# Earlier rounding of the first down weights, activations by token half, two sums postponed, and two gate stretches in the last attention pair

## The reference, cut to what matters

```
h = RMSNorm(x) * (1 + scale1) + shift1
p = h @ W_in
o_b = mixer_b(p slice)      b in {RG-LRU, stick-breaking attention, gated DeltaNet, RWKV-7}
x = x + gate1 * ( sum_b sigmoid(h W_gate_b + b_gate_b) * (o_b W_branch_b) ) @ W_out
h = RMSNorm(x) * (1 + scale2) + shift2
x = x + gate2 * ConvFFN(h)
out = RMSNorm(x)

ConvFFN(h) = (gelu(causal_conv3(h @ w_gate)) * (h @ w_up)) @ w_down      # 2816 hidden channels
```

## Time and profile before

| | |
|---|---|
| median of 3 runs | 1860.83 us (1860.56, 1860.83, 1863.67) |
| the profiled execution, its own time | 1862.51 us |
| its span, first to last instruction | 1860.7 us |
| mean granted TensorE clock | 0.995 |
| PE busy | 1821.3 us (98%) |
| DVE, POOL, ACT busy | 1132.7 (61%), 828.0 (44%), 589.1 us (32%) |

### The profile page before, as it was taken

How to read it: one execution, slowest core, us unless ns; L and a number is a source line. 1 busy time by engine, 2 the same in 40 slices (tenths; PEclk the granted TensorE clock), 3 DMA queues, 4 the chain that set the end, 5 groups by cost and what they waited for, 6 DMA issues and landing times.

```text
span 1860.7 us, 34460 instructions
## 1 busy us (share of the span) xinstructions
PE 1821.3 (98%) x14030; PEld 1458.8 (78%) x14030; DVE 1132.7 (61%) x1706; ACT 589.1 (32%) x957; POOL 828.0 (44%) x954
## 2 busy tenths in 40 slices
PE   6999999999999999999999999999999999999997
PEld 4778777767888888878878788878888888888885
DVE  4855568844555455465544653986666556665656
ACT  4341344352213122222131422543222332233223
POOL 2767556523242233222232747155454455455443
PEclk9999999999999999999999999999999999999999
DMA  9616211224120221230214551011022111111012
GB/s 339 221 46 237 91 62 57 87 95 128 50 91 25 87 95 39 76 104 35 78 55 174 190 215 46 23 46 59 33 68 68 45 45 45 68 45 58 33 68 91
DMA packets 72029, 163.55 MB, mean 88 GB/s; under 512 B 6112, under 2 KB 30816, under 8 KB 71904
## 3 DMA queue, kind: packets, MB, share of 16 engines
q1 hardware_dynamic: 64416, 142.88, 22.5%
q10 hardware_dynamic: 7488, 18.88, 2.6%
HBM read 133.17 MB, written 28.57 MB: 87 GB/s over the span
## 4 chain that ended last, share of the span: by engine, by line
PE 88%; DVE 6%; issue 2%; POOL 2%; ACT 1%; DMA 1%; SPq 1%; ACTq 0%; DVEq 0%; POOLq 0%
PE gbank L782 35%; PE gbank L1339 17%; PE mbank L1440 11%; PE mbank L1123 3%; PE mbank L1339 3%; PE gbank L1263 1%; PE gbank L1323 1%; PE gbank L1353 1%; PE mbank L1353 1%; DVE fa L2384 1%; POOL w_lo L650 1%; PE gbank L1123 1%; PE mbank L863 1%; PE mbank L1043 1%; PE gbank L884 1%
## 5 line engine op out<-in xcount | busy, mean ns | idle before, releaser
L646 POOL TENSOR_TENSOR w_hi<-w_raw,zero 128x256 fp32r<-128x256 f32 (+1 forms) x260 | 203.1, 811 | 618.7 <-PE gbank L782 598.1
L782 PE MATMUL gbank<-h_hi,w_hi 128*128 128x512 f32 x976 | 392.7, 402 | 0.2 <-POOL w_lo L650 0.2
L782 PE MATMUL gbank<-h_hi,w_lo 128*128 128x512 f32 x976 | 389.2, 399 | 0.0
L782 PE MATMUL gbank<-h_lo,w_hi 128*128 128x512 f32 x976 | 384.3, 394 | 0.0
L696 POOL TENSOR_TENSOR ra<-late,ra 128x256 fp32r<-128x256 f32 x208 | 187.8, 928 | 273.3 <-ACT ra L1926 273.3
L650 POOL TENSOR_TENSOR w_lo<-w_raw,w_hi 128x256 fp32r<-128x256 f32 (+1 forms) x260 | 252.7, 1002 | 5.1
L1440 PE MATMUL mbank<-ffn_a,ra 128*128 128x512 f32 x960 | 221.2, 391 | 3.5 <-POOL ra L696 2.9
L782 PEld LDWEIGHTS gbank<-h_hi,w_hi 128*128 128x128 f32 x976 | 183.7, 188 | 51.4 <-issue 14.3
L782 PEld LDWEIGHTS gbank<-h_hi,w_lo 128*128 128x128 f32 x976 | 183.5, 188 | 40.3 <-issue 0.7
L782 PEld LDWEIGHTS gbank<-h_lo,w_hi 128*128 128x128 f32 x976 | 183.9, 188 | 39.6 <-issue 2.8
L1440 PEld LDWEIGHTS mbank<-ffn_a,ra 128*128 128x128 f32 x960 | 181.2, 189 | 42.0 <-issue 4.3
(11 more groups left out here) (422 smaller groups left out, 2907.3 us busy)
## 6 DMA issues: line engine op xcount, KB each, us to landing
w_raw<-in_w_tail SPq DMA_DIRECT2D x72, 512.0 KB, 3.7
fa<-in_w_ada SPq DMA_DIRECT2D x48, 512.0 KB, 6.5
w_raw<-in_w_in SPq DMA_DIRECT2D x26, 512.0 KB, 4.2
p_scr<-fa ACTq DMA_DIRECT2D x20, 512.0 KB, 2.6
w_raw<-in_w_mix SPq DMA_DIRECT2D x16, 640.0 KB, 4.0
fa<-in_xT SPq DMA_DIRECT2D x16, 512.0 KB, 7.7
w_raw<-in_w_gate SPq DMA_DIRECT2D x16, 512.0 KB, 4.6
sig_scr<-fa ACTq DMA_DIRECT2D x32, 256.0 KB, 2.0
```

The lines of the kernel that those rows point to most:

```text
L646: last = pool.tensor_tensor(hi[:, c], raw[:, c], zero[:, 0:1].to_broadcast([P, w]), ALU.add)
L782: mm = pe.matmul(gb[bank], w, r, start=(q == 0), stop=(q == 3 * ks - 1))
```

## The change

- **Attention.** FILL_TAIL gets two more marks, 30 and 38, and the turn p == PAIRS puts gates(0, 30) between sb_turn(30) and sb_turn(31), and gates(0, 38) between sb_turn(31) and sb_values(15). The matmuls are taken out of the later gates(0, 48).
- **Weights.** On ACT, down_slot 0 and 1 move ahead of the four std_act_hi.
- **Activations by token half.** The single wait for all of e7 before std_act_hi becomes a wait for one e7 each. On DVE the two std_act_lo of token half 0 move ahead of std_mul of half 1. PE's new first_down makes m = 0 and m = 1 for half 0 first (after two act_lo), then both for half 1 (after four); ffn_down starts at m = 2 there.
- **Sums.** e7(0) and e7(2) write to two free half tiles (late 0 and 1) instead of over t12, so they need not wait for e6 and come first; e6(1), e6(3), e7(1), e7(3) follow, and e6(0) and e6(2) come last, after std_act_lo.

```diff
-FILL_TAIL, FILL_PRE = (6, 12, 18, 24), (48, 64, 76, 92, 110)
+FILL_TAIL, FILL_PRE = (6, 12, 18, 24, 30, 38), (48, 64, 76, 92, 110)
...
-                  "e6.0 e6.1 e6.2 e6.3 e7.0 e7.1 e7.2 e7.3 lo6.0 lo6.1 lo6.2 lo6.3 lo7.0 lo7.1 lo7.2 lo7.3"),
+                  "e7.0 e7.2 e6.1 e6.3 e7.1 e7.3 e6.0 e6.2 lo6.0 lo6.1 lo6.2 lo6.3 lo7.0 lo7.1 lo7.2 lo7.3"),
...
+        def e7_at(j):
+            return HT["12"][j] if j % 2 else late[:, j // 2, :]
...   PE, attention
+                if p == PAIRS:
+                    gates(0, FILL_TAIL[4])
                 if p:
                     sb_turn(2 * p - 1)
+                if p == PAIRS:
+                    gates(0, FILL_TAIL[5])
...   PE, FFN
+            def first_down():
+                pe.wait_ge(sem("s_lo"), SLOTS_A + 6)
+                pe.wait_ge(sem("c12"), 8)
+                for hf in range(2):
+                    pe.wait_ge(sem("act_lo"), 2 * hf + 2)
+                    for m in range(2):
+                        mm = down_half(5, m, hf)
+                        if hf == 1:
+                            mm.then_inc(sem("prod" if m else "half_done"), 1)
             second_tile(2, 5, 4, 3, 1)
+            first_down()
             ffn_down(0, 0, 5)
...   ACT
-            act.wait_ge(sem("e7"), at("e7", 3))
+            down_slot(0, 0, 0, 5)
+            down_slot(0, 0, 1, 5)
             for hf in range(2):
                 for t in range(2):
+                    act.wait_ge(sem("e7"), at("e7", 2 * t + hf))
                     std_act_hi(t, hf)
-            down_slot(0, 0, 0, 5)
-            down_slot(0, 0, 1, 5)
...   DVE
-            e6(0)
+            e7(0)
             s25(2, SLOTS_A + 2, Q[0], 0)
-            for j in range(1, 4):
+            e7(2)
+            for j in (1, 3):
                 e6(j)
+            for t in range(2):
+                std_act_lo(t, 0)
+            for j in (1, 3):
+                e7(j)
             std_mul(0, 1)
             std_mul(1, 1)
-            for j in range(4):
-                e7(j)
-            for hf in range(2):
-                for t in range(2):
-                    std_act_lo(t, hf)
+            for t in range(2):
+                std_act_lo(t, 1)
+            for j in (0, 2):
+                e6(j)
```

More of the change, by code:

```diff
@@ L1428, in ffn_down @@
                 n0 = i * SLOTS_G + (off * SLOTS_G + SLOTS_A + base)
-                pe.wait_ge(sem("act_lo"), i * 2 + (off * 2 + 4))
                 if off:
+                    pe.wait_ge(sem("act_lo"), i * 2 + (off * 2 + 4))
                     pe.wait_ge(sem("q_set"), i * 2 + (off * 2 + 1))
-                for m in range(KT):
+                for m in range(0 if off else 2, KT):
                     if m % 2 == 0:
@@ L1437, in ffn_down, with down_half @@
                     for hf in range(2):
-                        for k in range(2):
-                            for which, (w, r) in enumerate(down_part(SLOTS_A + base + m // 2, m, hf, k)):
-                                mm = pe.matmul(mb[m % 2 * 2 + hf], w, r, start=(k == 0 and which == 0), stop=(k == 1 and which == 2))
+                        mm = down_half(base, m, hf)
                     mm.then_inc(sem("prod" if m % 2 else "half_done"), 1)
+            def down_half(base, m, hf):
+                for k in range(2):
+                    for which, (w, r) in enumerate(down_part(SLOTS_A + base + m // 2, m, hf, k)):
+                        mm = pe.matmul(mb[m % 2 * 2 + hf], w, r, start=(k == 0 and which == 0), stop=(k == 1 and which == 2))
+                return mm
+            def first_down():
[7 more added lines that the diff above has]
+                            mm.then_inc(sem("prod" if m else "half_done"), 1)
             second_tile(2, 5, 4, 3, 1)
+            first_down()
             ffn_down(0, 0, 5)
@@ L1980, in hi7 @@
                 act.wait_ge(sem(freed[0]), at(*freed))
-                h_part("7", j, E[7][j][:, LO], HT["12"][j], hd[:, 16 + j:17 + j], "e7")
+                h_part("7", j, E[7][j][:, LO], e7_at(j), hd[:, 16 + j:17 + j], "e7")
             def std_gate(t, hf):
@@ L2816, in lo7 @@
             def lo7(j):
-                h_low("7", j, E[7][j][:, UP], HT["12"][j], hd[:, 16 + j:17 + j], E[7][j][:, LO])
+                h_low("7", j, E[7][j][:, UP], e7_at(j), hd[:, 16 + j:17 + j], E[7][j][:, LO])
             def e1(j):
@@ L2839, in e7 @@
             def e7(j):
-                dve.wait_ge(sem("e6"), at("e6", j))
-                dve.tensor_tensor(HT["12"][j], HT["21"][j], HT["22"][j], ALU.add).then_inc(done("e7", j), 1)
+                if j % 2:
+                    dve.wait_ge(sem("e6"), at("e6", j))
+                else:
+                    dve.wait_ge(sem("s_lo"), SLOTS_A + 2)
+                dve.tensor_tensor(e7_at(j), HT["21"][j], HT["22"][j], ALU.add).then_inc(done("e7", j), 1)
             def std_conv2(t, hf):
```

## The result

The changed kernel takes 1869.97 us (median of 6 runs, 1867.95 to 1870.85) against 1862.45 us for the kernel before (6 runs, 1860.56 to 1863.67): a ratio of 1.0041, with a 95% interval of 1.0031 to 1.0051. It is slower by 0.41%, and the forecast was no change (1861.6, range 1857.0 to 1864.5). The profiled execution of the changed kernel is its fastest run: 1867.95 us, with a span of 1866.2, that is 5.5 us over the span before. The median of the kernel before is now one of six runs; the forecast was laid on the first three (1860.83), 1.6 us lower.

The account below looks back on a forecast made before the run. PE, busy 98% of the span, was taken to bound the kernel. Attention's +2.0 us and the FFN start's -1.2 made +0.8 us, forecast 1861.6 us on the median 1860.83, range 1857.0 to 1864.5.

Parts of the forecast that it names:

- part 1: End of attention, the two gate stretches: +0.7 us for the later sums of tk and +1.3 for the clock, +2.0 us.
- that chain: End of attention, from the values through ACT's sb_hi(31), gate_raw(0), sigmoid and softplus to DVE's tk_g: 2.1 us later.
- tk's sums: PE's L974 at the end of attention, behind the wait for tk_g: at 423.4 instead of 422.66, +0.7 us.
- The slow clock behind the wait: After PE's 3.3 us wait for tk_g the clock falls to 1.2 GHz: 1.3 us taken, 0 to 1.7.
- old slow stretch: Low clock behind the two attention gaps in the kernel before: 3.4 us at 1.2 GHz, costing 1.7 us of work.
- Rival B: Attention: low clock after the tk_g wait lasts twice 3.4 us, timed runs lacked the old fall; 1865.0 us, chance 0.09.
- Part 2: FFN start, earlier weights and activations by token half: 2.6 us gained at m = 2, 1.4 lost to the clock, net -1.2.
- POOL beside five DVE instructions: FFN start: POOL's moved down slots slow DVE's first five sums and act_lo by 0 to 2.2 us, 1.0 taken.
- From lo6(0) to down_add(0): FFN start, on DVE: 4.2 us (3.3 to 5.13) instead of 5.13, since POOL has two slots fewer there.
- The gain at m = 2: FFN start: m = 2 begins at 1239.0 instead of 1241.58, 2.6 us gained (0.5 to 4.5).
- the clock's cost: FFN start: low clock behind the wait for down_add(0) falls on m = 2 to 7, 0 to 1.7 us, 1.4 taken.
- the rule: FFN start: DVE with two SBUF inputs and GpSimd exclude each other; m = 2 about 1 us later, net near zero.

Follow-up runs that it names:

- split_after_tkg: The changed kernel, with POOL waiting for tk_g before it splits the third gate unit; 1865.90 us, ratio 1.0014 to the kernel before.
- busy_wait: The changed kernel with 20 extra matmuls on PE, results unread, ahead of the wait for tk; 1865.83 us, ratio 1.0018 to the kernel before.
- ffn_only: The kernel before with only the FFN part of the change, attention as before; 1861.58 us, ratio 0.9996.
- after_again: The changed kernel run once more, beside other runs on one chip; 1869.59 us, ratio 1.0042 to the kernel before.
- adds_first2: The kernel before with only the FFN part of the change, and DVE's first six down_adds moved up; 1856.26 us, ratio 0.9969.
- adds_only: The kernel before with nothing of the change, only DVE's first six down_adds moved up; 1861.21 us, ratio 0.9995.

## Why the prediction was wrong

**The step that failed** is in part 1: "Nothing in that chain depends on the gates that were brought forward, so it moves as a whole". The gates brought forward end the 48th early, that frees a buffer, and POOL's split starts at 419.81, in the middle of the chain's small DVE steps, instead of behind it. The forecast followed semaphores up the chain and did not ask what an earlier 48th gate sets off. It cost 2.5 us: tk's sums moved by +3.25 where +0.7 was forecast, and split_after_tkg brings back the forecast's own 9.6 us and 3.1 us of wait.

**The slow clock behind the wait** was foreseen but mis-sized: 1.3 us forecast, 2.4 measured (busy_wait; 1.5 to 3.1 over five executions), since the stretch is 6.8 us and not the 3.4 of the earlier trace rows. That it costs nothing as far as it lies in the wait was right. Part 1 is thus 3.25 + 2.40 = 5.65 us against 2.0. Against an execution free of the old slow stretch (812.65 in ffn_only) it is 819.86 - 812.65 = 7.2 us, where the forecast had 3.3. Rival B had the low clock lasting twice 3.4 us, and that happened in every run with the gates in full but busy_wait; but two thirds of what part 1 cost beyond the forecast (2.5 of 3.65 us) are POOL's, which no rival had. That part 1 also lies beyond the 4.9 us from which rival B decides is chance: without POOL's 2.5 us it would be 3.1.

**Part 2** had the right mechanism. The wait for POOL went, m = 0 and 1 ran without a stall, m = 2 waited for down_add(0), and the clock fell on m = 2 to 7. The sizes were off. POOL beside five DVE instructions cost 5.47 - 3.1 = 2.4 us, where 1.0 was taken of 0 to 2.2, so std_act_hi, c12 and hi6(0) came 1.3 us later than forecast (1238.98 - 5.04 = 1233.94 in the time of the kernel before; forecast 1232.6). From lo6(0) to down_add(0) it was 4.43 us (forecast 4.2), and to m = 2 another 1.42 (forecast 1.41). The gain at m = 2 is 1.04 us instead of 2.6, the clock's cost 1.6 instead of 1.4, and the net +0.57 instead of -1.2 (+1.16 in after_again).

The Trainium skill, SBUF — State Buffer, in its section on the two separate sides, says that a DVE instruction with two SBUF inputs and a GpSimd one that reads SBUF contend for a shared port pair, which is locked for a whole instruction while the other engine blocks. The prediction weighed this for the FFN alone, by an estimate of about 1 us (m = 2 near 1240.0), and did not use it. Measured in that frame m = 2 came at 1245.58 - 5.04 = 1240.54. It had set the rule aside because it took POOL's instructions beside lo6 to last 0.89 us; but that is the mean of eight, and the first four, all begun before lo6, started 0.75 us apart. The other four, in the kernel before, took longer:

```profile
1234.93 4.15 POOL L696 TENSOR_TENSOR ra<-w_raw,ra 128x256 fp32r<-128x256 f32 x4
```

The rows after fit the rule too: the DVE instructions start 1.15 us apart and POOL's take 4.58 / 4 = 1.15, and the small steps of attention start 0.68 us apart beside POOL's 2.77 / 4 = 0.69. Each engine seems to let the other through once, which is taking turns and not the stretching that the prediction read.

**Sum.** Forecast +2.0 - 1.2 = +0.8; measured +5.65 + 0.57 - 0.61 = +5.6 in the two profiles. By the medians it is 7.5 us; after_again locates 1.5 of the other 2. The rest of the way from the forecast, 1861.6, is the 1.6 us by which the kernel before came out above the three runs it was laid on.

## What to carry to other kernels

When a step is brought forward, list also what its end sets free on engines that are off the chain, and look whether that work now lands beside the chain: here a weight split that had run in nobody's way slowed ten tiny DVE steps from 2.3 to 4.8 us. A wait that is removed pays only when the next in line is removed as well: three orders of the same adds put the stall at m = 2, at m = 6 and nowhere, and only the last one gained, since the other two each kept a stall of about 4 us and a slow clock with it. Filling gaps of half a microsecond on PE was worth nothing that these runs can tell, and filling them past what the next result needs made a wait of 5.6 us.

## What the runs showed of the hardware that was not expected

Six DVE instructions of 128x32 went from 0.18 and 0.19 us to between 0.53 and 0.65 us beside POOL. The tensor_scalar steps with a single tensor read suffer nearly as much as those with two; how the chip runs these was not tried.

The same code is followed by a slow clock in one execution and not in another. The unchanged end of attention, with the same gaps of 0.46 and 0.37 us, has 0.79 over 415 to 423 before and in adds_first2, and 1.00 in ffn_only and adds_only, which is worth 1.6 us of the first distance (814.2 against 812.65):

```profile
415.00:423.00 8.00, 8.00 (x40) 6.39 (x37) 4.00 (x22) 4.09 (x11) 2.05 (x4) 1.00 0.82 224
```

(The line is of ffn_only.) Around the end of the wait of 4.2 to 4.3 us for down_add(0) the clock was low for 3.4 us in two executions and for 6.8 in three. What decides it stays open.
